# Two-layer decoder trunk: the second feed-forward's first output projection in seven products instead of eight

## What is computed

```python
D_MODEL, SEQ = 1024, 1024
D_FF = ((8 * D_MODEL + 3 * 256 - 1) // (3 * 256)) * 256     # 2816

def swiglu(x, w_in, w_out):
    gate, up = jnp.split(x @ w_in, 2, axis=-1)
    return (jax.nn.silu(gate) * up) @ w_out

h = h + mix
h = h + swiglu(rmsnorm(h, norm_ffn[layer]), w_ffn_in[layer], w_ffn_out[layer])
```

## Time and profile before

| | us |
|---|---|
| median of 3 runs (2225.45 to 2225.85) | 2225.8 |
| profiled execution, its own time | 2225.23 |
| its span, first to last instruction | 2223.4 |
| PE busy | 2198.2 |
| DVE busy | 1674.6 |
| ACT busy | 1181.7 |
| POOL busy | 361.2 |

### The profile page before, as it was taken

The page is one execution under the profiler, slowest core; times in us unless marked ns, Lnnn a source line. Parts: engine busy times, 40 slices in busy tenths (PEclk is TensorE's granted clock), DMA queues, the critical chain, the costliest instruction groups (busy, mean ns, idle before and its releaser), DMA issues.

```text
span 2223.4 us, 28679 instructions
## 1 busy us (share of the span) xinstructions
PE 2198.2 (99%) x10393; PEld 1831.4 (82%) x10393; DVE 1674.6 (75%) x2353; ACT 1181.7 (53%) x1873; POOL 361.2 (16%) x352
## 2 busy tenths in 40 slices
PE   8999999999999999999999999999999999999998
PEld 6888887888888888887888888888888888888886
DVE  7667788787778777688666766775777778888866
ACT  5543576355555555356666666754535555555525
POOL 4000000022222222021111111102002222222200
PEclk9999999999999999999999999999999999999999
DMA  5110300366676666431111111132136666666652
GB/s 152 48 60 26 95 15 24 133 133 133 133 133 133 131 125 124 134 115 29 39 30 39 39 39 39 30 105 76 38 133 120 127 121 127 128 127 130 129 167 86
DMA packets 208984, 208.03 MB, mean 94 GB/s; under 512 B 9705, under 2 KB 153297, under 8 KB 208849
## 3 DMA queue, kind: packets, MB, share of 16 engines
q0 software_dynamic: 39168, 75.51, 20.7%
q1 hardware_dynamic: 167952, 126.43, 19.1%
q10 hardware_dynamic: 1728, 4.31, 0.7%
HBM read 122.28 MB, written 83.95 MB: 93 GB/s over the span
## 4 chain that ended last, share of the span: by engine, by line
PE 93%; DVE 4%; issue 1%; ACT 1%; DMA 0%; ACTq 0%; DVEq 0%
PE ps L1244 37%; PE ps L1049 18%; PE ps L1332 14%; PE ps L1445 10%; PE ps L1492 3%; PE ps L1583 3%; PE ps L1479 3%; PE ps L1460 1%; PE ps L1459 1%; PE ps L1562 1%; PE ps L1134 0%; PE ps L1525 0%; PE ps L1098 0%; PE ps L1417 0%; PE ps L1400 0%
## 5 line engine op out<-in xcount | busy, mean ns | idle before, releaser
L977 POOL DMA_DIRECT2D spill<-c x256 | 223.7, 926 | 725.5 <-DVE c L2705 493.2
L2574 DVE TENSOR_TENSOR ring_l<-raw_ffn,ring_h 128x512 fp32r<-128x512 f32 x320 | 222.8, 699 | 154.5 <-ACT ring_h L1811 153.1
L1811 ACT ACTIVATE ring_h<-raw_ffn 128x512 fp32r<-128x512 f32 x320 | 199.0, 626 | 196.5 <-PE ps L1244 103.7
L1904 ACT ACTIVATE c<-ps 128x512 f32<-128x512 f32 x256 | 150.2, 597 | 13.2
L1445 PE MATMUL ps<-xh,wh_att 128*128 128x512 f32 x368 | 148.6, 404 | 1.6 <-DVE wl_att L2276 1.6
L1811 ACT ACTIVATE ring_h<-w_sum 128x512 fp32r<-128x512 f32 x112 | 69.5, 625 | 147.2 <-PE ps L1049 38.9
L2169 ACT ACTIVATE probs<-ps,nmax 128x896 f32<-128x896 f32 (+7 forms) x128 | 95.0, 742 | 99.2 <-DVE nmax L3121 97.3
L1445 PE MATMUL ps<-xh,wl_att 128*128 128x512 f32 x368 | 143.9, 391 | 0.0
L1445 PE MATMUL ps<-xl,wh_att 128*128 128x512 f32 x368 | 143.9, 391 | 0.0
L3128 DVE TENSOR_TENSOR ptl<-ps,pth 128x512 fp32r<-128x512 f32 (+1 forms) x160 | 96.9, 634 | 52.4 <-ACT pth L2204 51.0
L2705 DVE TENSOR_TENSOR c<-ps,c 128x512 f32<-128x512 f32 x192 | 123.5, 685 | 4.8 <-PE ps L1332 4.3
(11 more groups left out here) (411 smaller groups left out, 6295.4 us busy)
## 6 DMA issues: line engine op xcount, KB each, us to landing
spill<-c POOLq DMA_DIRECT2D x256, 256.0 KB, 6.0
raw_ffn<-in_w_ffn_in SPq DMA_DIRECT2D x88, 512.0 KB, 5.3
raw_ffn<-in_w_ffn_out SPq DMA_DIRECT2D x44, 512.0 KB, 7.2
resid<-spill SPq DMA_DIRECT2D x24, 512.0 KB, 6.9
raw<-in_w_rec_in SPq DMA_DIRECT2D x16, 512.0 KB, 5.6
spill<-resid POOLq DMA_DIRECT2D x16, 512.0 KB, 2.9
raw_att<-in_w_kvf SPq DMA_DIRECT2D x16, 512.0 KB, 4.1
xin<-in_x SPq DMA_DIRECT2D x4, 1024.0 KB, 9.8
```

The costliest lines, as they stand in the source:

```text
L977: pool.dma_start(spill[m, :, half * BANK:(half + 1) * BANK], block[:, :], accum_op=ALU.add).then_inc(sem, 16)
L1811: act.activation(F.ring_h[slot][:, :], src, ACT.Copy).then_inc(F.unit_hi, 1)
L1904: act.activation(dst[:, :], y if what == "s5" else w, ACT.Copy).then_inc(out_tapped, 1)
L2574: dve.tensor_tensor(F.ring_l[slot][:, :], src, F.ring_h[slot][:, :].bitcast(F32), ALU.subtract).then_inc(F.unit_lo, 1)
```

## The change

In the second feed-forward (`F.f == 1`) group 1 is no longer plain: the output projection of group 0 is formed by `out_products`. It follows that:

- PE runs 84 matmuls instead of 96 there; group 1 has seven output units instead of four, with four sums of weights.
- ACT rounds B11, T1, B2, T2, T3 and T4 instead of two whole hidden blocks; it has 16 copies more (`out_tap`).
- DVE forms T1 to T4 and six low halves instead of two, and 12 joins instead of eight additions to the residual. T1 and B11 stand in `att_to_ffn`. In `group` the low half of unit P4 and the join C22 now stand ahead of gate times up (0, 1), behind which come the low half of T1 and the sums.
- POOL stores the residual right after the attention, no longer after group 1's tiles, and issues 16 adding DMAs for group 1.

The rest is bookkeeping: counts of units and semaphores take `F`, because the two feed-forwards now differ. The diff, cut to its core:

```diff
     tiles.plan("ffn1T", [2, 3] * 4).plan("ffn1E", [2, 3, 1, 0] * 2)
 
 
@@ -562,25 +562,25 @@
                 return g + 1
             return (g[0], g[1] + 1) if g[1] < UNROLL - 1 else (g[0] + 1, 0)
...
-        def is_plain(g):
+        def is_plain(F, g):
 
-            return isinstance(g, int) and g in (0, 1, LAST, GROUPS)
+            return isinstance(g, int) and (g in (0, LAST, GROUPS) or g == 1 and F.f == 0)
...
             def all_outputs(F):
                 for m in range(KT):
-                    slot, n = out_tile(F, 1, m)
+                    slot, n = resid_tile(F, m) if F.f else out_tile(F, 1, m)
                     pool.wait_ge(drained[slot], n)
                     pool.dma_start(spill[m], resid[:, m, :]).then_inc(added[m % 4], 16)
-                for g in range(2, LAST):
+                for g in range(2 - F.f, LAST):
                     add_outputs(F, g)
...
             def out_products(F, g):
 
+                if g == 1:
+                    for t in range(2):
+                        slot, count = first_tile(F, 1, t)
+                        pe.wait_ge(drained[slot], count)
...
                 if part in ("B11", "T1"):
-                    if g == 1:
+                    if g == 0:
+                        act.wait_ge(F.product_filled, B12_USED)
+                    elif g == 1 and F.f == 0:
                         act.wait_ge(out_filled, out_base(F, 1) + 8)
                     else:
                         act.wait_ge(out_product, out_at(F, g, 28, 28))
@@ -1982,7 +1986,12 @@
                     pair_high(F, g, 0, P4)
                     if F.f == 1:
                         tap(F, g, 0, "s5")
-                    hidden_high(F, prev, 1)
+                        h_part_high(F, g, "B2")
+                        h_part_high(F, g, "T2")
+                        h_part_high(F, g, "T3")
+                        h_part_high(F, g, "T4")
+                    else:
+                        hidden_high(F, prev, 1)
                 else:
                     pair_silu(F, prev, 1)
                     pair_high(F, g, 0, P5)
...
                 pair_high(F, 1, 0, P1)
                 pair_high(F, 1, 0, P2)
-                hidden_high(F, 0, 0)
                 pair_high(F, 1, 0, P6)
                 pair_high(F, 1, 0, P5)
                 tap(F, 1, 0, "s1")
+                h_part_high(F, 0, "B11")
                 pair_high(F, 1, 0, P7)
+                h_part_high(F, 0, "T1")
...
                 if part == "T1":
                     dve.wait_ge(h_ready, times(g, 2, 2 * F.f * GROUPS + 1))
-                    if g != 1:
+                    if g != 1 - F.f:
                         dve.wait_ge(h_part_lo, out_at(F, g, 6, 5))
+                    elif g == 0:
+                        dve.wait_ge(F.part_lo, F.part_lows.index(("T4", 2)) + 1)
                     ins = dve.tensor_tensor(t0, up0[:, BANK:S], up0[:, 0:BANK], ALU.subtract)
                 elif part == "T2":
                     dve.wait_ge(h_summed, out_at(F, g, 4, 1))
+                    if g == 1 and F.f == 1:
+                        dve.wait_ge(F.part_lo, F.part_lows.index(("T4", 3)) + 1)
+                        dve.wait_ge(h_ready, 2 * GROUPS + 2)
                     ins = dve.tensor_tensor(t1, up1[:, BANK:S], t0, ALU.subtract)
...
                     join(F, g, 0, "C11")
-                    gate_times_up(F, prev, 1)
-                    pair_low(F, g, 0, P4)
-                    join(F, g, 0, "C22")
-                    hidden_low(F, prev, 1)
+                    if F.f == 0:
+                        gate_times_up(F, prev, 1)
+                        pair_low(F, g, 0, P4)
+                        join(F, g, 0, "C22")
+                        hidden_low(F, prev, 1)
+                    else:
+                        pair_low(F, g, 0, P4)
+                        join(F, g, 0, "C22")
+                        gate_times_up(F, prev, 1)
+                        h_part_low(F, prev, "T1")
+                        h_sum(F, g, "T2")
+                        h_part_low(F, g, "B2")
+                        h_sum(F, g, "T3")
+                        h_part_low(F, g, "T2")
...
                     h_sum(F, g, "T4")
                     h_part_low(F, g, "T3")
                     weight_sum(F, g, "O", 1, 2)
-                    join(F, g, 0, "C22")
+                    if g != 1:
+                        join(F, g, 0, "C22")
                     h_part_low(F, g, "T4")
                     pair_low(F, g, "O", P1)
                     join(F, g, 0, "C12")
...
                 late_parts(F, "T4")
                 pair_low(F, 1, 0, P1)
                 pair_low(F, 1, 0, P2)
-                hidden_low(F, 0, 0)
                 pair_low(F, 1, 0, P6)
                 pair_low(F, 1, 0, P5)
+                h_sum(F, 0, "T1")
+                h_part_low(F, 0, "B11")
                 pair_low(F, 1, 0, P7)
                 weight_sum(F, 1, 0, 4)
```

More of the change, by code:

```diff
@@ L563, in after_group, with first_of, set_unit, unit @@
             return (g[0], g[1] + 1) if g[1] < UNROLL - 1 else (g[0] + 1, 0)
-        def is_plain(g):
-            return isinstance(g, int) and g in (0, 1, LAST, GROUPS)
-        def first_of(g, one, first, per):
+        def is_plain(F, g):
+            return isinstance(g, int) and (g in (0, LAST, GROUPS) or g == 1 and F.f == 0)
+        def first_of(F, g, one, per, less):
             if isinstance(g, int):
[L572 to L579, removed]
+                return 0, one + per * (g - 1) - less * ((g > 1 and F.f == 0) + (g > LAST))
+            return g[0] * (UNROLL * per), one + per * (g[1] + 1) - less * (F.f == 0)
+        def set_unit(F, g, j):
+            return {0: 0, "O": PRODUCTS, 1: PRODUCTS + (4 if is_plain(F, g) else PRODUCTS)}[j]
+        def unit(F, g, off):
             if isinstance(g, int) and g == 0:
                 return off % RING, off + 1
-            moving, fixed = first_of(g, UNITS_FIRST, UNITS_FIRST + 18, 21)
+            moving, fixed = first_of(F, g, UNITS_FIRST, 3 * PRODUCTS, 3)
             return (fixed + off) % RING, moving + (fixed + off + 1)
@@ L1256, in first_group @@
                     begun.update((tile, (tile, half)))
-                    product(F, bank(tile[0], half), unit(0, u), F.first_part(u, half), start, True, F.part_lows)
+                    product(F, bank(tile[0], half), unit(F, 0, u), F.first_part(u, half), start, True, F.part_lows)
                     if n == F.stat_after:
@@ L1262, in pair_products @@
                 w, x, y = banks(j)
-                off = set_unit(g, j)
+                off = set_unit(F, g, j)
                 lows = F.part_lows if isinstance(g, int) and g == 1 and j == 0 else None
-                behind = j == 1 and not is_plain(g)
+                behind = j == 1 and not is_plain(F, g)
                 if lows is not None:
@@ L1336, in out_group @@
             def out_group(F, g):
-                if is_plain(g):
+                if is_plain(F, g):
                     out_tiles_of(F, g)
@@ L1403, in token_epilogue @@
             def token_epilogue():
-                units = [unit(GROUPS, n) for n in range(RING)]
+                units = [unit(F1, GROUPS, n) for n in range(RING)]
                 def part(b, k):
@@ L2595, in weight_sum @@
                         if not (g == 1 and j == 0):
-                            dve.wait_ge(F.unit_lo, unit(g, P5 if g in (1, LAST) and j == 1 else at - PRODUCTS + P5)[1])
+                            dve.wait_ge(F.unit_lo, unit(F, g, P5 if is_plain(F, g) and j == 1 else at - PRODUCTS + P5)[1])
                         ins = dve.tensor_tensor(F.w_sum[0][:, :], u1, u2, ALU.add)
```

72 lines of the change are left out of this document (35 added, 37 removed).

## The result

| | before | after |
|---|---|---|
| median of 20 runs | 2225.86 us (2225.45 to 2226.81) | 2229.92 us (2229.11 to 2230.62) |
| profiled execution, its own time | 2225.23 us | 2229.12 us |
| its span | 2223.4 us | 2227.3 us |

The ratio is 1.0018, 95% interval [1.0012, 1.0024]: 4.1 us slower, 2.6 us above the forecast and inside the forecast range by 0.08 us. The sign was that of the forecast's own case; the size was that of a rival.

A forecast was written before the change was run, and what follows sets the result against it. TensorE, busy 2198.2 of 2223.4 us, was taken as the bound; 3.91 + 0.11 + 0.15 - 2.72 = +1.45 us gave a profiled 2226.7 us, and with the median 0.57 above the profiled execution 2227.3 us, range 2225.0 to 2230.0.

The forecast's parts named there:

- the forecast's own case: Whole kernel: the reckoned wait outweighs the saving, +1.45 us; 2226.3 to 2228.5 us, chance 0.60.
- the clock's case: Rival: granted clock falls in PE's new wait, costing 1.7 to 3.5 us more; 2229.0 to 2230.8 us, chance 0.14.
- a clock below 1.00 behind the seam: Sign of being wrong: granted clock under full after group 1's output projection begins on PE, 1625.75 us before the change.
- The saving: Group 1's output projection on PE: 96 matmuls become 84, twelve times 0.2267, 2.72 us less.
- The wait: First output product: DVE's chain from C22 takes 9.09 us, unit ready 1629.60, PE starts 3.91 us late.
- seven of the twelve instructions would have to be gone: Under the whole-gain rival (2223.1 us, chance 0.08): what DVE's chain must lose for the first unit to be in time.
- Loses 0.11 more: First matmul behind PE's wait at the first output product: 0.34 instead of 0.23 us, 0.11 us extra.
- 0.1 us short of that: Clock rival: clock fell about 4.0 us behind the program's last matmul; the reckoned new wait stays just below.
- half to all of that length: Clock rival's price: slow stretch of half to all of 6.9 us after program start, costing 1.7 to 3.5 us.
- 0.15 us more: Fourth output product: its first DVE join ends at 1638.0, PE needs it at 1637.93; 0.15 us added.
- What was put at nothing: Moved and added steps at no cost: residual stores on POOL (2.9 us each), ACT's work, adding DMAs, taps, joins.

The follow-up runs named there:

- e5: Changed kernel with gate times up (0, 1), T2, T3 and several low halves moved earlier, T4 and weight sums ahead of C22: 2223.19 us, ratio 0.9989.
- e2: Changed kernel with gate times up (0, 1) put back ahead of unit P4's low half and join C22: 2228.23 us, ratio 1.0012.
- e4: Changed kernel with both reorderings, that of e2 and that of e3, together: 2226.83 us, ratio 1.0006 against the kernel before.
- e6: Changed kernel with three more additions on VectorE that nobody reads, ahead of the first output unit's low half: 2232.42 us, ratio 1.0029.
- e0: The changed kernel again, unaltered, on the other chip beside e5 and e6: 2229.92 us, ratio 1.0019 against the kernel before.
- e1: Changed kernel with twelve dummy matmuls on TensorE ahead of its wait for the first output unit: 2227.88 us, ratio 1.001.
- e3: Changed kernel with the first output unit's halves ahead of T3's and T4's (low half also ahead of the weight sums): 2227.88 us, ratio 1.0011.

## Why the prediction was right, and where it was wrong

The median came to lie inside the range partly by luck: nine of the 20 executions took more than 2230.0 us, and the range reached that far only because it took in the lower half of the clock's case. One of the prediction's own signs of being wrong came true, "a clock below 1.00 behind the seam", and three of its figures failed: the 84 matmuls took 20.93 us and not 19.2, PE's busy time fell by 0.5 us and not by 2.7, and the second pair began at 1651.40 and not near 1649.

**The saving** of 2.72 us was taken 0.19 too high: twelve times 0.2267, where the 84 matmuls of such a projection take 19.23 us and not 19.04. The prediction itself expected "84 such matmuls in 19.2 us" and did not use it in the sum. e5 shows 2.57 in the medians.

**The wait**: right in place, releaser and mechanism, and close in size. Predicted were 9.09 us from C22's start to the unit and 3.91 us of delay; measured 9.31 and 4.33. Of the 0.42 missing, 0.22 is the chain: T4's sum came 0.79 us behind T2's low half, not 0.60. It is written over T2's block (`t_sum1_1<-up_second1,t_sum1_1`), which that low half reads until 1626.29, and starts at 1626.39; that it must wait for this end is argued from the order, not tried. The other 0.20 is PE's reaction, 0.26 us where the row of the first feed-forward showed 0.06; why it is longer here is not shown. The remark that seven of the twelve instructions would have to be gone counts them at 0.60 us; by the prediction's own prices the five longest make up 4.19 us, where 3.91 had to go. e2, e4, e5 and e6 confirm the mechanism in both directions: the time follows VectorE's order behind C22.

**"Loses 0.11 more"**: this is the step that failed. What PE pays behind the wait was 1.70 us in the profile, 2.24 in that of e0, and by an estimate from the medians about 2.0 (e1: 1.76, less 0.21 of reaction, plus the 0.47 that e1 itself pays), not 0.11. That is 1.9 of the 2.6 us by which the forecast was missed; 0.42 are the wait and 0.19 the saving. The clock's case was written down, and its times, 2229.0 to 2230.8 us, hold the measured one; its chance, 0.14, was too low. The step behind that chance read the program's tail as a threshold: a fall "about 4.0 us" behind the last matmul, the new wait "0.1 us short of that", hence a fall unlikely. One event gives a delay that happened, not a least delay. By the same measure, from the end of PE's last matmul, the runs show falls after 2.0 (e0), 2.3 (e2) and 3.0 us (e6), and one behind waits of 0.5 and 1.8 us (e4). Of seven profiled executions with a wait at this seam, five had a fall, at a different moment each. The mean clocks say that behind a wait of 3.0 us and more it fell in all 49 executions (0.998 or 0.997), where of the kernel before only 7 of 56 have 0.998. With the clock's case as its own, the forecast would have been 2229.0 or more. The price itself was reckoned well: "half to all of that length" is what was seen, 3.4 and 6.8 us, and "costs half its length" holds in all five to 0.1 us, with the slow stretch counted only where PE works.

**The rule that it cited**: the Trainium skill (TensorE: Matmul & The Clock Gate, "What's actually happening") says that the default state is throttled and that activity releases it; the prediction took from it that such a wait is paid twice. e1 agrees: with PE busy in the wait and its data no sooner there, 1.76 us are gone.

**"0.15 us more" at the fourth product**: in the changed kernel the trace shows no such wait; PE, slowed, came there later. In e1, at full clock, 0.16 us stand at that place; that the join holds PE there is argued from the order of the code.

**What was put at nothing**: the stores of the residual landed in 5.2 us each at the median, not 2.9, the last of them by 1583, 40 us ahead of need. ScalarE had no part in the wait. The adding DMAs held nobody up, and in group 2 there is no wait. These held.

**Ahead of the seam.** Most of the 0.39 us by which the second feed-forward starts later arises at the end of the attention, ahead of every step that the change edits:

```profile
1502.86 0.70 PE L1587 MATMUL ps<-xh,wh_att 128*128 128x512 f32 x2 [0.36 <-DVE xl L3119]
```

This `xl` follows a load of `rinv` by DMA. Before, the load was issued at 1492.86 and POOL went on with it at 1497.57, after 4.71 us; in the changed kernel these were 1493.01 and 1497.96, 4.95 us. So 0.15 us were there already when the load was issued and 0.24 came with it. PE has this wait, of 0.2 to 0.6 us, in the changed kernel, e0, e1, e2, e3, e4 and e6, and not in the kernel before and e5, where the load took 4.71 and 4.72 us; in the seven others it took 4.82 to 5.21. (e5's second feed-forward starts 0.42 us later all the same, because 0.41 were there at the load's issue.) The prediction had no term for it. Whether the change brings it or chance does stays open: the kernel before has one profile, and e5's median gains the full 2.57 us.

## What to carry to other kernels

What an edit saves on the bounding engine can be lost again where a helper delivers too late. So count the helper's unbroken run behind the last thing that it has to wait for (here C22) against the moment when the bounding engine wants the result. Then look for the helper's idle time one stage earlier: the same instructions, moved there, gave the whole gain. If an edit makes a TensorE wait that was busy, forecast the wait twice, once as idle time and once as a stretch at 1.2 GHz: here every execution with a wait of 3.0 us or more paid both, and of those with two waits of at most 1.8 us nearly half. A single fall seen elsewhere in a trace is no least length. To tell the two apart, fill the wait with dummy matmuls: what is gained without the release moving is the clock's part, less what the reaction changes (0.21 us here).

## What the runs showed of the hardware

- The clock fell from 2.4 to 1.2 GHz in five profiled executions at 1628.28 (e0), 1628.86 (e2), 1629.88 (e6), 1631.14 (the changed kernel) and 1632.90 us (e4), inside the wait or behind it. It stayed low for 3.4 us (the changed kernel, e4) or 6.8 us (e0, e2, e6), also where PE was back at work for most of that time. In the profile of e3, with waits of 1.67 and 1.78 us, it did not fall. By the mean clock of each execution it fell in all 49 with a wait of 3.0 us or more, in 5 of 11 of e4 (0.52 and 1.78 us) and in 4 of 11 of e3.
- At 1.2 GHz 512-column matmuls start 0.427 us apart, at 2.4 GHz 0.227.
- PE's reaction, from the end of VectorE's instruction to the start of the matmul, was 0.26 to 0.30 us at the first output product, behind waits of 0.52 (e4), 1.67 (e3), 3.02 (e2), 4.17 (the changed kernel, e0) and 6.63 us (e6), and 0.05 to 0.06 us behind the dummies (e1) and at the second output product (e3, e4, waits of 1.78 us). So it does not go by the length of the wait; what it goes by is not shown.
